# Two zero strips instead of a spread tile, two weight pieces kept between parts, and eight more row slots for the last gather of v

## The reference

```
h = rms_norm(x) * (1 + sc1) + sh1
q, k, v, qi, ki, wi, cu = split(h @ w_in[l])       # w_in[l]: 1024 x 3144
x = x + g1 * (concat(attention(q, k, v, qi, ki, wi), conv(cu)) @ w_out[l])
h2 = rms_norm(x) * (1 + sc2) + sh2
e, g = router(h2 @ peer_wq[l], peer_sub_keys[l])   # 128 experts and gates of each token
coef = g * gelu(sum_d peer_u[l][e] * h2)           # one number for each token and expert
x = x + g2 * sum_k coef[k] * peer_v[l][e[k]]
```

## Time and profile before

| | us |
|---|---|
| median of 3 runs | 1887.08 |
| lowest and highest run | 1879.58, 1896.24 |
| span of the profiled execution, first to last instruction | 1733.4 |
| busy in that span: PE, DVE, POOL, ACT | 1039.2, 1103.2, 1015.9, 273.4 |

### The profile page before, as it was taken

How to read it: one execution, slowest core, us unless ns; L and a number is a source line. 1 busy time by engine, 2 the same in 40 slices (tenths; PEclk the granted TensorE clock), 3 DMA queues, 4 the chain that set the end, 5 groups by cost and what they waited for, 6 DMA issues and landing times.

```text
span 1733.4 us, 18207 instructions
## 1 busy us (share of the span) xinstructions
PE 1039.2 (60%) x6158; PEld 590.6 (34%) x6158; DVE 1103.2 (64%) x3003; ACT 273.4 (16%) x717; POOL 1015.9 (59%) x1133
## 2 busy tenths in 40 slices
PE   7979897406896588603788569611689610005555
PEld 4547674303363156301345146500236200001111
DVE  1987989996218576888117676889513979991000
ACT  2141235202110035300101024400210100000000
POOL 2610435676655763566755664567655777776774
PEclk8989899657998799655899679765899865557888
DMA  9998999999999999999999999999999999999998
GB/s 373 393 368 327 405 405 383 409 409 409 409 409 407 408 404 410 397 410 397 410 409 409 394 409 408 399 407 409 406 406 402 391 410 410 409 410 389 409 409 330
DMA packets 195481, 691.98 MB, mean 399 GB/s; under 512 B 21360, under 2 KB 21376, under 8 KB 195134
## 3 DMA queue, kind: packets, MB, share of 16 engines
q0 software_dynamic: 147840, 537.06, 78.1%
q1 hardware_dynamic: 47550, 153.77, 22.8%
HBM read 689.71 MB, written 1.05 MB: 398 GB/s over the span
## 4 chain that ended last, share of the span: by engine, by line
DMA 41%; PE 24%; DVE 15%; POOL 13%; issue 6%; ACT 1%; SPq 0%; DVEq 0%; ACTq 0%; POOLq 0%
DMA rows<-in_peer_v,v_at 20%; DMA rows<-in_peer_u,u_at 18%; PE ps L921 8%; DVE rows L1586 8%; PE ps L876 7%; POOL rows L698 7%; POOL rows L690 6%; DMA kiw<-in_w_in 1%; PE ps L818 1%; PE ps L864 1%; PE ps L848 1%; DMA rows<-in_w_ada 1%; DVE rows L1568 1%; PE ps L735 1%; PE ps L804 1%
## 5 line engine op out<-in xcount | busy, mean ns | idle before, releaser
L690 POOL DMA_INDIRECT rows<-in_peer_u,u_at x512 | 482.5, 942 | 370.8 <-DVE dots L1586 202.5
L1586 DVE CUSTOM_DVE_ANT_0 rows<-rows,ps 128x1024 f32<-128x1024 f32 x512 | 610.3, 1219 | 92.5 <-DMA rows<-in_peer_u,u_at 78.6
L698 POOL DMA_INDIRECT rows<-in_peer_v,v_at x512 | 485.7, 949 | 283.9 <-PE ps L921 153.4
L921 PE MATMUL ps<-rows,spread_c 128*32 128x512 f32 x2048 | 325.7, 764 | 215.0 <-DMA rows<-in_peer_v,v_at 215.0
L735 PE MATMUL ps<-ident 128*128 128x128 f32 x228 | 39.9, 346 | 354.3 <-DVE dots L1586 354.3
L921 PEld LDWEIGHTS ps<-rows,spread_c 128*32 128x32 f32 x2048 | 71.4, 125 | 414.8 <-issue 412.6
L735 PEld LDWEIGHTS ps<-ident 128*128 128x128 f32 x228 | 35.6, 183 | 369.8 <-DVE dots L1586 356.6
L876 PEld LDWEIGHTS ps<-hT,wring 128*128 128x128 f32 x1152 | 137.0, 199 | 25.7 <-issue 24.1
L876 PE MATMUL ps<-hT,wring 128*128 128x128 f32 x1152 | 142.2, 285 | 0.0
L848 PE MATMUL ps<-wring,hT 128*128 128x512 f32 x256 | 117.1, 600 | 8.3 <-DMA wring<-in_w_in 7.5
L902 PE MATMUL ps<-diag_eq,hc 128*128 128x128 f32 x744 | 104.7, 307 | 25.3 <-ACT diag_eq L1274 25.2
(11 more groups left out here) (254 smaller groups left out, 1183.9 us busy)
## 6 DMA issues: line engine op xcount, KB each, us to landing
wring<-in_w_in SPq DMA_DIRECT2D x34, 1024.0 KB, 13.2
wring<-in_w_ada SPq DMA_DIRECT2D x31, 1024.0 KB, 10.6
wring<-in_peer_wq SPq DMA_DIRECT2D x28, 1024.0 KB, 9.6
rows<-in_w_ada SPq DMA_DIRECT2D x16, 1024.0 KB, 14.9
wring<-in_w_out SPq DMA_DIRECT2D x13, 1024.0 KB, 17.1
rows<-in_peer_u,u_at POOLq DMA_INDIRECT x512, 14.1
rows<-in_peer_v,v_at POOLq DMA_INDIRECT x512, 9.5
rows<-in_w_in SPq DMA_DIRECT2D x6, 1024.0 KB, 15.9
```

The source lines that it names most:

```text
L690: pool.indirect_dma_start(row(n), None, u_rows, bass.IndirectOffsetOnAxis(ap=u_at[:, p % 2, k:k + 1], axis=0)).then_inc(row_landed[n % SLO ...
L698: pool.indirect_dma_start(row(n), None, v_rows, bass.IndirectOffsetOnAxis(ap=v_at[:, p % 2, tok:tok + 1], axis=0)).then_inc(row_landed[n % ...
L921: ins = pe.matmul(ps[32 * g:32 * g + 32, YB + q, :], spread_c[:, g, a, :], row(n)[:, q * 512:q * 512 + 512], start=a == 0, stop=a == 31)
L1586: dve.tensor_tensor_reduce(out=row(n), in0=row(n), in1=h2_shown, scale=1.0, scalar=0.0, op0=ALU.mult, op1=ALU.add, accum_out=dots[:, k:k + ...
```

## The change

It does four things.

- `window`, a new tile of 128 x 2 x 4 x 63 float32, is zero but for its column 31. Group a of parts 0 to 2 takes the strip a % 2, puts its coefficients into column 31 and reads the 32 columns from 31 - a: so the coefficients stand in column a of what PE reads. DVE writes the coefficients of groups 0 and 1 and copies the turned coefficients to `coef`; POOL puts the others (a = 2 to 31) between its gathers, each after the gather 4a + 8, which waits for group a - 2 (`put_window`). PE waits for `window_ready` before each group from 2 on. POOL clears `window` at the start.
- `spread_c` is used for coefficients only in the last part; ACT clears it in part 3, once the projection has been read.
- The first two pieces of `vqi` of part 2 go to the two halves of `spread_c` and stay there for part 3, which doesn't load them (`STAYED`).
- The last gather of v has 21 slots: eight more in `wring` (`MORE`), taken ahead of the others.

```
+STAYED = {(("vqi", 3), h): (("vqi", 2), h) for h in range(2)}
...
-    uses = [(n, h) for n in blocks for h in range(pieces(n))]
+    uses = [(n, h) for n in blocks for h in range(pieces(n)) if (n, h) not in STAYED]
...
+        elif (name, h) in STAYED.values():
+            slot = KEPT[h]
...
+        last_v = v_item(PARTS - 1, 0)
+        row_slot, row_turn, row_before, holds = [], [], [], {}
+        line = collections.deque(range(SLOTS))
+        for n in range(PARTS * 2 * P):
+            if n == last_v:
+                line.extendleft(range(SLOTS + MORE - 1, SLOTS - 1, -1))
+            s = line.popleft()
+            line.append(s)
+            row_before.append(holds.get(s))
+            holds[s] = n
...
         def wait_slot_free(eng, n):
 
+            if last_v <= n < last_v + MORE:
+                slot = (n - last_v) // 2
+                wait_weight_used(eng, max(i for i, s in enumerate(slot_of) if s == slot))
...
-            if n >= SLOTS:
-                p, i = divmod(n - SLOTS, 2 * P)
+            if row_before[n] is not None:
+                p, i = divmod(row_before[n], 2 * P)
...
+            seq_(pool.memset(window[:, :, :, :], 0.0))
...
+            def put_window(p, a):
+                if a == 2:
+                    pool.wait_ge(coef_turned, p + 1)
+                seq_(pool.tensor_copy(window[:, a % 2, :, 31], coef[:, a:P:32]), window_ready)
...
+                    if p and k == 4:
+                        put_window(p - 1, 31)
...
+                    if p + 1 < PARTS and m >= 16 and m % 4 == 0:
+                        put_window(p, m // 4 - 2)
+                if p + 1 < PARTS:
+                    pool.wait_ge(v_used, p * P + 116)
+                    put_window(p, 30)
...
+                    if p + 1 < PARTS and a > 1:
+                        pe.wait_ge(window_ready, 30 * p + a - 1)
...
-                            ins = pe.matmul(ps[32 * g:32 * g + 32, YB + q, :], spread_c[:, g, a, :],
+                            c = window[:, a % 2, g, 31 - a:63 - a] if p + 1 < PARTS else spread_c[:, g, a, :]
+                            ins = pe.matmul(ps[32 * g:32 * g + 32, YB + q, :], c,
...
-                if p == 0:
-                    wait_full(act, ("v", 1))
+                if p + 1 == PARTS:
+                    wait_full(act, ("qi", p))
...
+                if p + 1 < PARTS:
+                    if p:
+                        dve.wait_ge(v_used, p * P)
+                    seq_(dve.tensor_copy(window[:, 0, :, 31], o[:, 0:P:32]))
+                    seq_(dve.tensor_copy(window[:, 1, :, 31], o[:, 1:P:32]), spread_ready)
+                    give(dve.tensor_copy(coef[:, :], o[:, 0:P]), name)
+                    dve.sem_inc(coef_turned, 1)
```

More of the change, by code:

```diff
@@ L28 @@
 SLOTS = 13
+MORE = 8
 HB, YB = 4, 6
@@ L338, in trunk @@
         spread_c = sb("spread_c", [P, 4, 32, 32])
+        window = sb("window", [P, 2, 4, 63])
         kiw = sb("kiw", [P, KT, DH + NI])
@@ L477, in trunk @@
         v_at_ready = sem("v_at_ready")
-        row_landed = [sem(f"row_landed{s}") for s in range(SLOTS)]
+        row_landed = [sem(f"row_landed{s}") for s in range(SLOTS + MORE)]
         u_used = sem("u_used")
@@ L485, in trunk @@
         spread_cleared = sem("spread_cleared")
+        coef_turned = sem("coef_turned")
+        window_ready = sem("window_ready")
         x_done = sem("x_done")
@@ L538, in row @@
         def row(n):
-            return rows[:, n % SLOTS, :]
+            s = row_slot[n]
+            if s < SLOTS:
+                return rows[:, s, :]
+            return wring[:, (s - SLOTS) // 2, (s - SLOTS) % 2 * D:((s - SLOTS) % 2 + 1) * D]
         def wait_row(eng, n):
-            eng.wait_ge(row_landed[n % SLOTS], 16 * (n // SLOTS + 1))
+            eng.wait_ge(row_landed[row_slot[n]], 16 * row_turn[n])
+        last_v = v_item(PARTS - 1, 0)
[8 more added lines that the diff above has]
+            holds[s] = n
+            row_slot.append(s)
+            row_turn.append(row_slot.count(s))
         def wait_slot_free(eng, n):
+            if last_v <= n < last_v + MORE:
+                slot = (n - last_v) // 2
+                wait_weight_used(eng, max(i for i, s in enumerate(slot_of) if s == slot))
             if n < 12:
@@ L625, in _ @@
                     done_small = True
-                if use_before[i] is not None:
+                if (name, h) in STAYED.values():
+                    b, n = bank(("v", 1))
+                    sp.wait_ge(full[b], n)
+                elif use_before[i] is not None:
                     wait_weight_used(sp, use_before[i])
@@ L691, in _ @@
                                             bass.IndirectOffsetOnAxis(ap=u_at[:, p % 2, k:k + 1], axis=0)
-                                            ).then_inc(row_landed[n % SLOTS], 16)
+                                            ).then_inc(row_landed[row_slot[n]], 16)
+                    if p and k == 4:
+                        put_window(p - 1, 31)
                 pool.wait_ge(v_at_ready, p + 1)
@@ L713, in piece @@
                     next_is("block", name)
-                i = use_at[(name, h)]
+                i = use_at[STAYED.get((name, h), (name, h))]
                 pe.wait_ge(w_landed[slot_of[i]], 16 * use_number[i])
@@ L850, in proj_wide @@
                             ins.then_inc(full[b], 1)
-                    if h < 3:
+                    if (name, h) in piece_count:
                         ins.then_inc(piece_used, 1)
@@ L1927, in coefficients @@
                 o = wait_full(dve, name)
-                if p:
-                    dve.wait_ge(v_used, p * P)
+                if p + 1 < PARTS:
[5 more added lines that the diff above has]
+                    dve.sem_inc(coef_turned, 1)
                 else:
                     dve.wait_ge(spread_cleared, 1)
-                diagonal = spread_c[:, :, :, :].rearrange("p g a c -> p g (a c)")[:, :, 0:1024:33]
-                give(dve.tensor_copy(diagonal, o[:, 0:P].rearrange("p (g a) -> p g a", g=4)), name)
-                dve.sem_inc(spread_ready, 1)
+                    diagonal = spread_c[:, :, :, :].rearrange("p g a c -> p g (a c)")[:, :, 0:1024:33]
+                    give(dve.tensor_copy(diagonal, o[:, 0:P].rearrange("p (g a) -> p g a", g=4)), name)
+                    dve.sem_inc(spread_ready, 1)
             first(0)
```

## The result

The changed kernel takes 1901.59 us (median of 21 runs, 1888.81 to 1914.81), the kernel before 1888.92 us beside it (21 runs, 1878.79 to 1902.86). The ratio is 1.0067, 95% interval [1.0047, 1.0087]: slower by 0.7%, where 1.8 us less were forecast.

The account below looks back on a forecast made before the run. DMA transfers were taken as the bound, one row per 1.28 us. Weights -5.1, slots 0, copies +3.0, PE's wait 0 and small edits +0.3 gave -1.8 us: 1885 us, range 1871 to 1901 us.

Parts of the forecast that it names:

- What bounds the kernel: Whole kernel: DMA transfers at about 409.5 GB/s set the pace, one gathered row per 1.28 us; POOL only 0.04 us under it.
- The weights: Part 3 loads two vqi pieces fewer, so gathers for u in 1000 to 1140 us come earlier: -5.1 us.
- my two ends: Limits for the saved loads: 5.1 us gained, or 0 if DVE's own work holds that stage.
- The third rival: Saved loads were hidden behind DVE's work while the copies' 3 us stay: 1890 us, chance 0.08.
- The slots: Last v: eight more slots let POOL issue on to row 20, but rows land no earlier: 0, at best 2.3 us gained.
- a dip in which the landings don't stall: Last v, 1570 to 1585 us: DMA slows, worth 2.3 us of transfers, yet rows still land every 1.276 us.
- POOL's copies: v of parts 0 to 2: 90 copies at 0.28 us, mostly absorbed by waits and reserve: +3 us, ends 0 and 11.
- POOL becomes the pace of v: v of parts 0 to 2: DVE stretches copies to 0.6 us, losing 15 us in all: 1897 us, chance 0.17.
- PE's wait: PE's new wait for strips in v: short and few, costing 0, with up to 3 us as the end.
- The small edits: POOL's clearing, DVE's copies for the first groups, ACT's moved clearing, SP's new wait: +0.3 us for three parts.
- The range: Forecast limits of 1871 to 1901 us, reaching to 0.6 us a copy and a few us beyond the cases.

Follow-up runs that it names:

- the second measurement: The whole change, unmodified, timed again on a chip against the kernel before: 1904.84 us, ratio 1.0110.
- the idle copies: Kernel before plus 90 waited POOL copies among the gathers of v, into a tile nobody reads: 1.0108, and 1.0097 when repeated.
- the doubled copies: The whole change with each of POOL's 90 coefficient copies made twice in a row, both waited for: 1893.75 us, 1.0015 against the kernel before.
- four strips: The change without kept pieces and extra slots, with four strips instead of two, so coefficients are put four groups ahead: 1926.37 us, 1.0109 against the kernel before.
- the baseline: Profile of the kernel before with only an unused 2 KB scratch tile declared: span 1892.2 us; timed 1890.00 us, ratio 1.0010.
- The kernel before once more: The kernel before, unchanged, profiled in one further run: 1901.0 us, span 1899.2 us.
- the quick execution: The earlier profile of the unchanged kernel before, on which the prediction rests: span 1733.4 us, quicker than any timed run.

## Why the prediction was wrong

**What bounds the kernel: wrong for the executions that are timed.** "One row lands every 1.28 us whatever the engines do" holds in the earlier trace rows, and not in the others. There DMA rests for 93 us, and the stages of u wait for the layer's chain. The sign stood in the front: 153.7 us between median and span, which I took for time outside the span. It is 1.8 us. What made one execution 8% quicker is open; its granted clock was 0.792, that of the others 0.742 to 0.764.

**The weights, -5.1 us: did not reach the path.** The queue moved 151.67 MB as forecast. But the stage in which most of those bytes were missing didn't shorten, and leaving the two loads out of the kernel before gave 0.9993 [0.9973, 1.0013], -1.3 us. I took the whole of my two ends on the strength of DVE's 27.9 us of waits for rows; in the timed executions DVE waits there for ACT and the layer's chain. The third rival, "the change doesn't reach the path", named this, and I gave it 0.08.

**The slots, 0: right.** 1.0007 alone. The reason was only partly right: I spoke of a dip in which the landings don't stall. With 21 slots the wait moves behind row 20, since all slots wait for the coefficients, here 10.8 us behind the last dot.

**POOL's copies, +3.0 us: the step that failed.** The price of one was right or too high: 0.20 us, and 0.17 us of added pause instead of the 0.28 us that I put in. 8 of the 90 took longer, 0.30 to 1.23 us. The longest, on POOL and on DVE:

```profile
1422.94 1.23 POOL L715 COPY window<-coef 128x4 f32<-128x4 f32 x1
```

```profile
1422.90 1.22 DVE L1571 CUSTOM_DVE_ANT_0 hb<-xs 128x1024 f32<-128x1024 f32 x1
```

That is the price of the rival "POOL becomes the pace of v", at 8 copies and not at 90; the mean was 0.235 us, below the 0.33 us from which it decides. The Trainium skill, "SBUF — State Buffer", section "Who interferes with whom", says that a DVE instruction with two inputs in SBUF contends with a GpSimd instruction that reads SBUF. The trace agrees: L1571 takes `xs` as both inputs, and the two end together, at 1424.2 and 1424.1.

Yet by the ratios the change cost 13 us (21 in the second measurement), the idle copies 21 and 18 us, where +3.0 stood in the sum, and not by their time: with twice the time the change stands at 1.0015, with a pause of 0.06 us at 0.9998. A linear reckoning, so much pause less so much reserve, cannot give that. My forecast and my rival were both such reckonings; the rival's 1897 us came near the 1901.59 us measured by luck, since the doubled copies refute its reason.

**PE's wait, 0: its cost right, its size wrong.** PE waits 52.7 us in 20 pieces for strips, not a few short ones. It isn't what costs: with four strips the loss stays (1.0109), idle copies without any such wait lose as much, and in the doubled form, which is 11 us quicker than the change on the same chip, PE waits 45.7 us for the strips in 413 to 1520 us, against 34.2 us.

**The small edits, +0.3 us:** not measured apart. With the pause changed the whole change stands at 0.9998 and 1.0015. If those pauses are free themselves, which 1.0027 and 1.0013 for the idle copies leave open, all else in the change sums to between -5 and +7 us by the intervals.

**The range.** Its upper end, 1901 us, lay 0.6 us under the measured 1901.59. It went by a rival whose mechanism is refuted.

**What stays open** is why a pause of 0.17 us behind every fourth gather loses 0.5 to 1.1%, and pauses of 0.06 and 0.68 us next to nothing. Four gathers and one such pause take 4 x 1.245 + 0.17 = 5.15 us, and four rows at 409.5 GB/s 5.12 us: POOL would then issue just as DMA drains. That two periods fall together is worked out, not tested, and the timed executions seldom have that pace: over the whole v of part 1 a row comes every 1.73 us (222.0 us for 128). A row of pauses of 0.1, 0.3 and 0.4 us would test it. Whether the late starts of an engine behind another's result have a part in it wasn't tested either. Nor is it settled how a pause in v lengthens the stages of u by 2 to 4 us.

## What to carry to other kernels

Compare the span of a profile with the timed runs before a single row of it is used. If 8% lie between them, the profile is of another regime, and its bound (here a DMA that hardly rests) may not be that of the timed runs. A saving of bytes in a stage whose DMA share isn't full may be worth nothing, as here at 0.94; multiply length by share, stage by stage. And on the engine that issues gathers, a small instruction is not priced by its duration: time it in two or three lengths, since an unwaited copy can be free where the same copy, waited for, costs 0.7 to 1.1% of the kernel.

## What the runs showed that was not expected

- 90 idle copies between the gathers of u make the kernel before faster: 0.9952 [0.9929, 0.9975] and 0.9958 [0.9939, 0.9976] on two chips, 8 to 9 us. It is the quickest kernel of this study, and why is open. In its profile u and v of parts 1 and 2 last 870.1 us together, in the baseline 880.3 us.
- A waited copy of 128 x 4 on POOL costs 0.20 us and 0.27 us until the next gather; a second one behind it starts 0.06 us after the first ends; unwaited, the gather follows after 0.16 us.
- The granted clock of PE doesn't order the kernels: 0.755 in the span of 1876.4 us, 0.743 in 1892.2, 0.748 in 1902.9, 0.764 in 1899.0.
- In two places the profiles like the timed executions have PE idle for long before the product of `brow`, for the most part with no releaser named: 86.0 us in the kernel before once more, 78 to 90 us in all others but those of the idle copies in u, which have 55.4 and 55.6 us and are the quickest. In the quick execution all waits of PE for that product sum to 2.3 us. Whether this is how those copies gain is open. The kernel before once more (total us, times, longest):

```profile
PE ps L752 <- issue: 86.0, 2, 52.6
```
